# Token lists of the last four experts loaded once, and the last turn over the four slots written out

## Time and profile before

| | |
|---|---|
| median of three runs | 2112.06 us |
| profiled execution | 2113.34 us |
| its span | 2111.6 us |
| mean granted TensorE clock | 0.918 |
| PE busy | 82% of the span |
| queue of SP (q1) | 461.36 MB, 55.0% of sixteen engines' span |

### The profile page before, as it was taken

The page is one execution under the profiler, slowest core; times in us unless marked ns, Lnnn a source line. Parts: engine busy times, 40 slices in busy tenths (PEclk is TensorE's granted clock), DMA queues, the critical chain, the costliest instruction groups (busy, mean ns, idle before and its releaser), DMA issues.

```text
span 2111.6 us, 39341 instructions
## 1 busy us (share of the span) xinstructions
PE 1727.4 (82%) x13682; PEld 943.4 (45%) x13683; DVE 550.8 (26%) x1225; ACT 284.8 (13%) x614; POOL 399.8 (19%) x503
## 2 busy tenths in 40 slices
PE   7999999979999999999476576677777777776674
PEld 4576556644444444455333233444444443443342
DVE  5619223431122323255511011011111111110015
ACT  4011313311211111111100000000000000000002
POOL 1961002072151241001110011111111111110113
PEclk9999999999999999999688788899899988988787
DMA  6330411001111101562689999999999999999997
GB/s 206 144 63 6 149 40 46 20 20 40 50 40 36 54 30 34 187 262 90 272 337 427 426 411 408 369 379 381 396 406 401 409 407 417 411 410 413 421 397 265
DMA packets 109411, 511.11 MB, mean 242 GB/s; under 512 B 34016, under 2 KB 65248, under 8 KB 84256
## 3 DMA queue, kind: packets, MB, share of 16 engines
q1 hardware_dynamic: 78704, 461.36, 55.0%
q0 software_dynamic: 8816, 27.02, 3.5%
q10 hardware_dynamic: 21840, 22.06, 3.1%
HBM read 479.84 MB, written 34.35 MB: 244 GB/s over the span
## 4 chain that ended last, share of the span: by engine, by line
PE 53%; DMA 35%; DVE 4%; issue 4%; SPq 1%; ACTq 1%; ACT 1%; POOLq 1%; POOL 0%; DVEq 0%
DMA gain_b<-xf_rows,gather_idx 15%; PE act_bank L1059 14%; DMA tokens<-expert_token_table 13%; PE act_bank L829 13%; PE dve_bank L1059 6%; PE dve_bank L1124 5%; PE act_bank L1214 4%; DMA unit_results<-lane_row 3%; PE dve_bank L836 2%; PE act_bank L1226 2%; PE dve_bank L829 2%; DMA unit_results<-spatialT 2%; DMA unit<-in_w_in 1%; ACTq L1468 1%; PE dve_bank L1226 1%
## 5 line engine op out<-in xcount | busy, mean ns | idle before, releaser
L836 PE MATMUL dve_bank<-ident,gain_b 32*128 32x32 f32 x808 | 76.1, 239 | 230.5 <-DMA gain_b<-xf_rows,gather_idx 230.5
L1226 PE MATMUL act_bank<-unit,gain_a 128*32 128x256 f32 x2432 | 198.0, 481 | 26.1 <-DVE gain_a L2007 12.9
L2005 DVE TENSOR_TENSOR gain_a<-gain_a,act_bank 128x128 f32<-128x128 f32 x100 | 28.8, 288 | 707.1 <-ACT gain_a L1456 707.1
L1214 PE MATMUL act_bank<-unit,gain_a 128*32 128x256 f32 x3200 | 193.6, 396 | 20.3 <-issue 19.4
L836 PEld LDWEIGHTS dve_bank<-ident,gain_b 32*128 32x128 f32 x808 | 66.8, 157 | 275.4 <-issue 275.4
L1059 PE MATMUL act_bank<-norm_store,unit 128*128 128x512 f32 x384 | 170.5, 597 | 10.8 <-issue 10.8
L778 POOL COPY gather_idx<-tokens 32x1 int32 x100 | 17.7, 177 | 758.2 <-DMA gain_b<-xf_rows,gather_idx 529.0
L1214 PEld LDWEIGHTS act_bank<-unit,gain_a 128*32 128x32 f32 x3200 | 107.9, 115 | 110.6 <-issue 55.2
L1456 ACT ACTIVATE gain_a<-act_bank 128x128 f32<-128x128 f32 x101 | 28.0, 278 | 884.1 <-PE act_bank L1214 857.8
L1226 PEld LDWEIGHTS act_bank<-unit,gain_a 128*32 128x32 f32 x2432 | 90.6, 132 | 90.5 <-issue 67.5
L1059 PE MATMUL act_bank<-unit,unit 128*128 128x512 f32 x288 | 127.5, 592 | 0.0
(11 more groups left out here) (309 smaller groups left out, 1981.4 us busy)
## 6 DMA issues: line engine op xcount, KB each, us to landing
unit<-in_w SPq DMA_DIRECT2D x112, 2048.0 KB, 37.3
norm_store<-in_w SPq DMA_DIRECT2D x32, 2048.0 KB
mid_store<-in_w SPq DMA_DIRECT2D x32, 2048.0 KB, 34.5
rows_store<-in_w SPq DMA_DIRECT2D x16, 2048.0 KB, 45.1
unit<-in_w_gate SPq DMA_DIRECT2D x12, 1024.0 KB, 5.1
unit<-in_w_in SPq DMA_DIRECT2D x4, 2048.0 KB, 8.0
unit_results<-unit POOLq DMA_DIRECT2D x4, 2048.0 KB, 13.4
unit_results<-lane_row ACTq DMA_DIRECT2D x200, 32.0 KB
```

The source lines that it names most:

```text
L836: ins = nc.tensor.transpose(bank[:, n * rows:(n + 1) * rows], block_, ident[0:rows, 0:rows])
L1214: ins = nc.tensor.matmul(act_bank[0][h * CAP:(h + 1) * CAP, 0:2 * FQ].rearrange("t (w n) -> t w n", w=2), xT[:, k], w13[s][:, :, k, h * FQ ...
L1226: ins = nc.tensor.matmul(y_bank[s][z * CAP:(z + 1) * CAP, 0:DQ], hidT[:, j], w2s[s][:, j, z * DQ:(z + 1) * DQ], start=j == 0, stop=j == QU ...
L2005: v.tensor_tensor(hid, silu_g, act_bank[0][:, FQ:2 * FQ], ALU.mult).then_inc(per_slot["hid_ready"][s], 1)
```

## The change

- The token lists of the last four experts get a place of their own, `last_tokens`, in a part of `gain_a` that the expert stage leaves free. SP loads the four lists once, ahead of its refills, after a wait for `table_filled`; each list costs a `value_load` and a 4 KB DMA. In the last turn `refill` leaves the list out (`listed=False`), and POOL waits for `last_tokens_loaded`.
- `each_unit` loops over 15 turns, and the last turn over the four slots is written out behind the loop. PE, DVE and ACT read its bounds before the loop begins (`ahead=True`): twelve loads each, and four more on ACT for the rows of the results. POOL reads them in the last turn itself (`ahead=False`).
- On POOL `first` is no longer handed to `expert_tokens`, which loads it a second time for each slot in every turn.
- SP's refills of the last turn are written out as well.

```diff
+        last_tokens = gain_a[0:CAP, 640:640 + SLOTS * COLS].bitcast(I32).rearrange("t (s n) -> t s n", s=SLOTS)
...
-        def each_unit(eng, body, enter=None):
-
-            with eng.Fori(0, TURNS) as t:
+        def span_of(eng, at):
+            return (eng.value_load(spans[0:1, 0, at], min_val=0, max_val=SLOT_UNITS),
+                    eng.value_load(spans[0:1, 1, at], min_val=0, max_val=SLOT_UNITS),
+                    eng.value_load(spans[0:1, 2, at], min_val=0, max_val=2 * UNITS))
+
+        def position(e):
+            return slice(e, e + 1)
+
+        def each_unit(eng, body, enter=None, ahead=True):
+
+            def units(s, t, span, own):
+                first, end, shift = span
+                with eng.Fori(first, end) as c:
+                    body(c, s, in_sequence(c, shift), t, own)
+
+            if ahead:
+                last_spans = [span_of(eng, position(e)) for e in last_of]
+                last_owns = [enter(s, TURNS - 1, position(e)) if enter else None for s, e in enumerate(last_of)]
+            with eng.Fori(0, TURNS - 1) as t:
                 for s in range(SLOTS):
                     at = bass.ds(t * SLOTS + s, 1)
...
+                    span = span_of(eng, at)
+                    units(s, t, span, enter(s, t, at) if enter else None)
+            for s, e in enumerate(last_of):
+                if ahead:
+                    units(s, TURNS - 1, last_spans[s], last_owns[s])
+                else:
+                    span = span_of(eng, position(e))
+                    units(s, TURNS - 1, span, enter(s, TURNS - 1, position(e)))
...
+            sp.wait_ge(table_filled, 16 * 2 * NT)
+            for s, e in enumerate(last_of):
+                last_expert = sp.value_load(spans[0:1, 4, position(e)], min_val=0, max_val=E - 1)
+                sp.dma_start(last_tokens[:, s], table_of[bass.ds(last_expert, 1)].rearrange("e p n -> (e p) n")
+                             ).then_inc(last_tokens_loaded, 16)
...
-            with sp.Fori(1, TURNS) as t:
+            with sp.Fori(1, TURNS - 1) as t:
                 for s in range(SLOTS):
-                    refill(t * SLOTS + s, s)
+                    refill(bass.ds(t * SLOTS + s, 1), s)
+            for s, e in enumerate(last_of):
+                refill(position(e), s, listed=False)
...
-            def expert_tokens(s, t, first):
-                pool.wait_ge(tokens_loaded[s], (t + 1) * 16)
+            def expert_tokens(s, t, at):
+                first = pool.value_load(spans[0:1, 0, at], min_val=0, max_val=SLOT_UNITS)
+                if isinstance(t, int):
+                    pool.wait_ge(last_tokens_loaded, 16 * SLOTS)
+                else:
+                    pool.wait_ge(tokens_loaded[s], (t + 1) * 16)
                 pool.nop(nofuse=True)
-                return first
-
-            each_unit(pool, unit_work, expert_tokens)
+                return first, last_tokens if isinstance(t, int) else tokens
+
+            each_unit(pool, unit_work, expert_tokens, ahead=False)
```

More of the change, by code:

```diff
@@ L344, in program @@
         tokens_loaded = [sem(f"tokens_loaded{s}") for s in range(SLOTS)]
+        last_tokens_loaded = sem("last_tokens_loaded")
         units_known, order_known = sem("units_known"), sem("order_known")
@@ L589, in _, with refill @@
             expert_up(up, 3, halves=(1,))
-            def refill(e, s):
-                first = sp.value_load(spans[0:1, 0, bass.ds(e, 1)], min_val=0, max_val=SLOT_UNITS)
-                chosen_expert = sp.value_load(spans[0:1, 4, bass.ds(e, 1)], min_val=0, max_val=E - 1)
+            sp.wait_ge(table_filled, 16 * 2 * NT)
[3 more added lines that the diff above has]
+                             ).then_inc(last_tokens_loaded, 16)
+            def refill(at, s, listed=True):
+                first = sp.value_load(spans[0:1, 0, at], min_val=0, max_val=SLOT_UNITS)
+                chosen_expert = sp.value_load(spans[0:1, 4, at], min_val=0, max_val=E - 1)
                 up, down = expert(bass.ds(chosen_expert, 1))
                 sp.wait_ge(per_slot["hid_ready"][s], first)
-                sp.dma_start(tokens[:, s], table_of[bass.ds(chosen_expert, 1)].rearrange("e p n -> (e p) n")
-                             ).then_inc(tokens_loaded[s], 16)
+                if listed:
+                    sp.dma_start(tokens[:, s], table_of[bass.ds(chosen_expert, 1)].rearrange("e p n -> (e p) n")
+                                 ).then_inc(tokens_loaded[s], 16)
                 expert_up(up, s)
@@ L785, in gather, with unit_work @@
                                         bounds_check=T - 1, oob_is_err=False).then_inc(tok_gathered, 16)
-            def unit_work(c, s, u, t, first):
+            def unit_work(c, s, u, t, own):
+                first, lists = own
                 column = nc.s_assert_within(c - first, 0, COLS - 1, skip_runtime_bounds_check_because=(
                     "an expert has at most T tokens"))
-                gather(tokens[:, s, bass.ds(column, 1)], u)
-            def expert_tokens(s, t, first):
-                pool.wait_ge(tokens_loaded[s], (t + 1) * 16)
+                gather(lists[:, s, bass.ds(column, 1)], u)
+            def expert_tokens(s, t, at):
[4 more added lines that the diff above has]
+                    pool.wait_ge(tokens_loaded[s], (t + 1) * 16)
                 pool.nop(nofuse=True)
-                return first
-            each_unit(pool, unit_work, expert_tokens)
+                return first, last_tokens if isinstance(t, int) else tokens
+            each_unit(pool, unit_work, expert_tokens, ahead=False)
             units = (pool.value_load(spans[0:1, 1, E - 1:E], min_val=0, max_val=SLOT_UNITS)
@@ L1469, in unit_work, with result_rows @@
                                   y_rows[s][z * CAP:(z + 1) * CAP]).then_inc(per_slot["y_stored"][s], 16)
-            def result_rows(s, t, first):
-                return act.value_load(spans[0:1, 3, bass.ds(t * SLOTS + s, 1)], min_val=0, max_val=2 * UNITS)
+            def result_rows(s, t, at):
+                return act.value_load(spans[0:1, 3, at], min_val=0, max_val=2 * UNITS)
             gate(1)
```

## The result

The changed kernel takes 2118.57 us in the median of 14 runs (2113.07 to 2122.98). The kernel before, run beside it, takes 2111.49 (2107.50 to 2113.57, 14 runs). The ratio is 1.0034, with a 95% interval of 1.0025 to 1.0043: 5.3 to 9.1 us slower, 7.1 by the medians. The forecast was 2117.3, or +5.2, in a range of 2113.7 to 2121.2. The profiled execution took 2121.19, its span 2119.3.

What follows compares the result with a forecast made beforehand. The expert stage was taken as a byte-bound weight stream started by the first refill. 7.8 + 0.6 - 3.2 = +5.2 us on the profiled 2113.34 made 2118.5, for the median 2117.3; range 2113.7 to 2121.2.

Steps and rivals of the forecast that it cites:

- PE's twelve loads: Start, between PE's first token turn and first up product: twelve bound loads at 0.65 us delay the stream 7.8 us.
- the start is covered after all: Rival, chance 0.11: PE's loads overlap queued work or cost only 0.30 each; front costs about 4, sum near +1, 2113.
- POOL's second load: Before the first gather: loading `first` again costs 0.6 us; the other 59 run under gathers and cost nothing.
- A start that comes later moves everything by as much: Expert stage: its start is set by the first refill, and a start d later moves everything behind it by d.
- A middle that lets less than a third of the delay through: Rival, chance 0.09: holes in the mid-stream absorb the front delay, leaving only the end's gain, -3.2, 2108.9.
- DVE's loads: Start: DVE's twelve loads, 6.4 to 9.0 us, run beside PE's loads and the 5.46 us product; cost nothing.
- ACT's loads and SP's lists: Start: ACT's sixteen loads delay slot 1's refill, still in time; SP's lists, about 4 us, fit its pause; cost nothing.
- The last turn's order: Last turn, units A (slot 1), B, C (slot 2), D (slot 3): weights bind; D's copy 3.1 to 5.3 us sooner.
- The gain at the end: Last turn: D's copy comes sooner, its store meets the h rows; 3.2 us won, bounds 0.7 and 5.3.
- The end gives nothing back: Rival, chance 0.15: D's earlier stores wait on engines carrying h rows until 2068; only 0.7 won, +7.7, 2119.8.
- Fetching new code: Rival, chance 0.10: a code fetch for the written-out last turn stalls PE; some 5 us on top, 2122.3.

Runs made afterwards that it cites:

- pe_loads12: Kernel before with only PE's twelve number loads added, between its first token turn and first up product; 2119.13 against 2111.59 us, ratio 1.0031.
- bounds_late: Changed kernel with the last turn's bounds read in that turn on every engine; early lists and written-out turn stay; 2112.48 us, ratio 1.0000.
- all_early: Changed kernel with bound reads of PE, DVE and ACT moved ahead of their first steps, POOL's second load left out; 2108.93 against 2111.59 us, ratio 0.9993.
- pe_loads24: Kernel before with twenty-four number loads added on PE, between its first token turn and first up product; 2125.64 us, ratio 1.0072.
- dve_loads12: Kernel before with only DVE's twelve number loads added, behind its first token step; 2113.38 against 2112.89 us, ratio 1.0004.
- pe_early: Changed kernel with only PE's twelve bound reads moved ahead of its wait for the first gather; 2113.30 against 2110.62 us, ratio 1.0009.
- act_loads16: Kernel before with only ACT's sixteen number loads added, behind its first gate; 2112.09 us, ratio 1.0003.
- lists_only: Kernel before with only the last four token lists loaded early; PE, DVE and ACT keep their loop of 16 turns; 2110.39 against 2110.62 us, ratio 0.9995.
- rows_thin: all_early with only the first 64 columns, a sixteenth, of each h row loaded, so work is left out; 2107.31 us, ratio 0.9976.
- rows_after_stores: all_early with SP issuing the h rows and last gain only when slot 3's last stores have landed; 2119.38 against 2112.89 us, ratio 1.0038.

## Why the prediction was right, and the term that was off

- **PE's twelve loads, 7.8 us.** Right in place and size: 7.75 more idle time in the changed kernel, the same 9.69 in `pe_loads12`. The rival in which the start is covered after all is out: the loads begin at 1057.5, just behind the start of the turn (1057.44), but those of before began just behind theirs as well (1054.9 and 1054.64), so nothing more is saved.
- **POOL's second load, 0.6.** Right: the idle time before its first copy is 10.20 against 9.64 before, 10.22 in `bounds_late`, and 9.65 in `all_early`, which has no second load.
- **A start that comes later moves everything by as much.** Right within the intervals: 7.75 us of added idle time in `pe_loads12` cost 6.5 (4.4 to 8.7), and 15.47 in `pe_loads24` cost 15.2 (12.2 to 18.2). The hole at 1424, the last down weights and the last landing moved with the start. A middle that lets less than a third of the delay through is out; a loss of 2 or 3 us on the way isn't excluded.
- **DVE's loads, nothing.** Right in the changed kernel, for the reason given: they run beside PE's loads and the product behind them. Without PE's loads that cover is 2.8 to 3.0 us too short, by the traces of `dve_loads12` and `pe_early`. In the time this can't be shown.
- **ACT's loads and SP's lists, nothing.** Right: slot 1's refill came 11.48 us behind slot 0's (11 forecast), and `act_loads16` shows that this doesn't reach the end. The first refill of `lists_only` came 6.24 after its first product (6.32 before), so SP's four lists fit into its pause.
- **The last turn's order.** Nearly right. Moved by the 10.1 us of the first refill, B's product was due at 2044.7 (2045.14 measured), D's gather at 2051.8 (2052.93), D's up product at 2061.6 (2064.25), and D's copy between 2068.9 and 2071.1 (2071.17). Most of the delay is TensorE's: B's product took 6.37 instead of 5.5, C's down product 3.62 instead of 1.93. The 1.93 was that of B's down product; C's took 3.62 in the trace of before as well (its row is in the last section), so this part could have been read there. To the landing of the last down weights D's copy came 2.2 us closer (7.7 to 5.5), less than the 3 to 5 that the text named.
- **The gain at the end, 3.2: the term that was mis-sized.** The prediction put it as "D's store now meets the tail of the h rows in the queue, which costs part of it again: I take 3.2, with bounds 0.7 [...] and 5.3". It measured 2.6 at the copy and 1.0 at the first pick, near the lower bound (1.8 and 0.4 in `pe_early`). The mechanism was named, but no row priced D's own store: the 10.50 and 2.76 of the earlier trace rows stood there for B's stores, and 3.2 was taken near the lower end of what the copy was to win, 3.1 to 5.3. That left at most 2.1 us for a store that starts earlier, when the queue is fuller. The store took 4.38 instead of 2.76, and the wait behind the rows grew from 1.3 to 2.9, by the measure of `rows_thin` and `rows_after_stores`. With the measured terms the sum is 7.75 + 0.56 - 1.0 = +7.3 (+7.9 with the 0.4 of `pe_early`), against +7.1 by the medians. The gains at the end are readings of single executions; in the times alone the end can't be told from nothing won.
- **The rivals.** "The end gives nothing back" (+7.7) came closest, and the measured interval, 5.3 to 9.1, holds it, while the forecast's +5.2 just misses it; that the forecast's range held is owed to the front cost. What this rival got right is the place: the first pick comes about when SP's queue is empty, between 0.6 ahead of the last landing and 1.7 behind it in eleven profiles. The Trainium skill (DMA: Bandwidth & Descriptors, Queues, rings and completion order), which has a DMA engine take its queues in turn, fits with a store that is slowed while rows are queued; the order within an engine no row shows. "Fetching new code" is out at the 5 us that it named: the trace has three such transfers between 1990 and 2075 (before one), but PE's idle times from 2000 on end on weights, gathers and DVE, and `bounds_late`, with the same written-out turn, costs nothing that can be measured.

## What to carry to other kernels

In this kernel a load of a number costs PE about 0.65 us in the order of its program, of which its record shows 0.30. So put such loads where the engine already waits for something, and count what stands behind them on every engine that gets them: with PE's moved, DVE's were late. Ahead of this stream, which is bound by bytes, a delay went to the end about one for one, so a preparation that saves a little per turn at the end must cost less at the start. And a step that ends earlier is worth only what the transfer behind it keeps: look at what still fills the DMA engines at that moment, and price its store by that, not by its time in the trace of before.

## What the runs showed that was not expected

The first up product took 5.06 us in the changed kernel, 5.46 before and 6.41 in `pe_loads24`. The table by stretch of `pe_loads24` shows why it can vary: the granted clock.

```profile
1062.00:1071.00 9.00, 0.00 (x0) 0.00 (x0) 0.00 (x0) 0.00 (x0) 0.00 (x0) 0.50 0.00 0
1071.00:1074.00 3.00, 2.38 (x24) 1.22 (x28) 0.00 (x0) 0.00 (x0) 0.00 (x0) 0.50 0.03 5
1074.00:1077.00 3.00, 3.00 (x32) 1.42 (x28) 0.00 (x0) 0.00 (x0) 0.00 (x0) 0.50 0.00 0
1077.00:1080.00 3.00, 2.26 (x36) 1.36 (x32) 0.99 (x3) 0.28 (x1) 0.54 (x1) 0.96 0.01 1
```

After the idle time the clock stands at 0.50 (1.2 GHz) and rises only near 1077, more than 5 us into the product; in the changed kernel it stood at 0.50 up to 1070, 2 us into the product, at 0.82 in the three us behind that, and at 1.00 from 1073. The same happens to B's up product in the last turn of the changed kernel: TensorE waits 5.86 us for its weights, and the stretch of 2045 to 2048 is granted 0.50.

```profile
2042.00:2045.00 3.00, 0.00 (x0) 0.00 (x0) 0.00 (x0) 0.00 (x0) 0.00 (x0) 0.81 1.03 388
2045.00:2048.00 3.00, 2.86 (x28) 1.57 (x32) 0.00 (x0) 0.00 (x0) 0.18 (x1) 0.50 0.99 417
```

The kernel before lost this at another place: PE's wait, for the gather that the list had held up, came ahead of a down product, as its timeline shows. The stretch of 2032 to 2035 was granted 0.50, and that of 2035 to 2038 0.58.

```profile
2033.75 3.64 PE L1226 MATMUL act_bank<-unit,gain_a 128*32 128x256 f32 x32
2037.44 3.67 PE L1214 MATMUL act_bank<-mid_store,gain_a 128*32 128x256 f32 x64
...
2051.09 3.62 PE L1226 MATMUL act_bank<-unit,gain_a 128*32 128x256 f32 x32
```

So the wait for a list was exchanged for a wait for weights, and the slow stretch moved from a product of 32 matmuls (3.64 instead of 1.93, 1.7 lost) to one of 64 (6.37 instead of 3.67, 2.7 lost). By the lengths of these products that takes 1.0 us off the gain at the end, and no wait shows it; that all of it reached the copy isn't shown. C's down product, the last row above, is slow in both kernels.
